# Delta rule: the masked blocks of the inversion levels made by GpSimd into two buffers, one level ahead

## The chip, the cores and the metric

The kernel runs on one core of one Trainium2 chip. The metric is the device time of one execution in microseconds (us). Engines are called PE (TensorE), DVE (VectorE), ACT (ScalarE), POOL (GpSimd) and SP (SyncE, which issues nearly all DMAs).

## The reference, cut to what matters

The whole program is two transformer blocks in fp32 on 256 tokens (gated linear attention, a feed-forward, stick-breaking attention, a mixture of experts, then a second block with a chunked gMLP beside a gated delta rule, a feed-forward, latent attention and a feed-forward). The change touches the gated delta rule alone, which runs over 512 tokens (256 of context, 256 of the sequence), four heads, in two directions:

```python
gcum = jnp.cumsum(gc, axis=-1)
decay = jnp.exp(jnp.where(tri_incl, gcum[..., :, None] - gcum[..., None, :], -jnp.inf))
a_mat = jnp.where(tri_strict, jnp.einsum('nbhid,nbhjd->nbhij', kb, kc) * decay, 0.0)
t_mat = lax.linalg.triangular_solve(eye + a_mat, eye, lower=True, unit_diagonal=True)
u = jnp.einsum('nbhij,nbhjd->nbhid', t_mat, vb)
```

The kernel inverts the unit triangular matrix block by block. It begins with 2x2 blocks and doubles the block size in five levels. A level takes the entries of the matrix that belong to it (a multiplication by a 0/1 mask), forms products with the inverse so far, and subtracts them.

## The kernel before, in words

The 512 tokens are four tiles of 128, and each direction (a `Strand`, d = 0 or 1) takes them in four steps, in its own order. Four heads lie side by side, as 64x64 blocks on two halves of the partitions. So a masked block is a 128x256 fp32 tile.

Three generators work for each strand:

- `prepare(x)` builds the matrix of a step with products on PE (L2318, L2365, L2380), DVE multiplications (L2337, L2327 in threes, L2372), GpSimd multiplications (L2358 and L2359 for the start `UM`, L2387 for the attention block) and ACT copies (L2346, L2393 for the start `TM`). The result goes to `x.pairs[step % 2]`. Its marks (the semaphore counts reached) are kept in `x.prepared[step]`.
- `invert(x)` runs the five levels. A level has: the masked block X; the first products X by TM (L2428, 16 matmuls a strand on PE, recorded as such); the ACT copy XT (L2437); the second products (L2462, L2465); two DVE subtractions (L2481 and L2483, or L2481 and L2486 twice at level 5). The mask multiplication of the next level stands on DVE (L2452) beside the ACT copy: it waits for the first products, since there is one buffer X, and its result is waited for by `after_all` in front of the second products and in front of the next first products. The mask of level 1 of the next step is made there too, if `x.prepared` already holds that step when the code reaches that point; if not, `masked` (L2410) makes it at the start of the step, followed by a `yield`.
- `follow(x)` carries the state: POOL L2507 and L2508, PE L2514, L2532, L2565, L2581, L2597, L2613, L2635 with DVE and ACT steps between them. L2565 needs the finished inverse of its step.

`side_by_side` takes the eight generators (the last two are `tail_norm`) in the order invert 0, invert 1, follow 0, follow 1, prepare 0, prepare 1, tails, and runs each to its next `yield`, round after round. The instruction order of every engine is the order in which this loop reaches the instructions, and each engine executes its queue in order. Taking out or adding one `yield` shifts a generator against the others by one round, on all engines. The generators of strand 1 begin three rounds later (`STAGGER`).

`after_all` waits for the latest count of each engine in the own generator's chain (`chain[-1]`); `adopt` adds other marks to it. Two waits in `prepare` use the global count: PE L2365 waits for `dve_done.n`, so for every DVE instruction emitted before it by any generator; DVE L2372 waits for `pe_done.n` in the same manner.

No weights are consumed in this stage. The DMA queue of SP has filled the ring before it and waits.

Of the kernel before, what the change touches and what calls it, by code (L numbers as in the profile page):

```python
# [15 lines left out]
ALU = mybir.AluOpType  # L16
# [47 lines left out]
def build(nc, stream, params, where, out):  # L64
# [4 lines left out]
    with ExitStack() as ctx:  # L69
# [3 lines left out]
        def sem(name):  # L73
            return ctx.enter_context(nc.semaphore(name))
# [17 lines left out]
        chain = [{}]  # L92
        tile_used = Done(sem("tile_used"), chain)
        pe_done = Done(sem("pe_done"), chain)
        act_done = Done(sem("act_done"), chain)
        dve_done = Done(sem("dve_done"), chain)
        pool_done = Done(sem("pool_done"), chain)
        everyone = (tile_used, pe_done, act_done, dve_done, pool_done)

        def after_all(eng):  # L100


            for d in everyone:
                n = d.n if len(chain) == 1 else chain[-1].get(d, 0)

                if n and not (len(chain) > 1 and eng.engine == nc.tensor.engine and d in (tile_used, pe_done)):
                    eng.wait_ge(d.sem, n)
# [17 lines left out]
        def c(name, a=0, b=None):  # L125
            off, n = where[name]
            return par[:, off + a:off + (n if b is None else b)]
# [18 lines left out]
        block = ctx.enter_context(nc.Block())  # L146
# [164 lines left out]
        def wait_marks(eng, marks):  # L311
            for d, n in marks:
                eng.wait_ge(d.sem, n)
# [1554 lines left out]
        W = GH * P  # L1868
# [17 lines left out]
        def marks_here():  # L1886
            return [(d, n) for d, n in chain[-1].items() if n]
# [4 lines left out]
        def adopt(*lists):  # L1892
            for marks in lists:
                for d, n in marks:
                    chain[-1][d] = max(chain[-1].get(d, 0), n)
# [371 lines left out]
        compact = lambda x: x.rearrange("p (h n) -> p h n", h=GH)  # L2267
        small_both = lambda m: m.unsqueeze(1).to_broadcast([P, GH, HB])
        ident_c = c("ident_c")
        CW = GH * HB  # L2270
# [124 lines left out]
                yield  # L2395

        def invert(x):
            X, TM = x.xt[:, 0:CW], x.xt[:, CW:W]
            UM, XT = x.ul[:, 0:CW], x.ul[:, CW:W]

            @block.gpsimd
            def _(pool):
                after_all(pool)
                pool_done.by(nc.gpsimd.memset(x.full, 0.0))

            def masked(step, lev):
                @block.vector
                def _(dve):
                    after_all(dve)
                    dve_done.by(nc.vector.tensor_tensor(compact(X), compact(x.pairs[step % 2][:, 0:CW]), x.level(lev), ALU.mult))  # L2410

            ahead = False
            for step in range(T4):
                while len(x.prepared) <= step:
                    yield
                adopt(x.prepared[step])
                if not ahead:
                    masked(step, 1)
                    yield
                for lev in range(1, 6):  # L2420
                    UM0, TM0 = (x.start[:, 0:CW], x.start[:, CW:W]) if lev == 1 else (UM, TM)

                    @block.tensor
                    def _(pe):
                        after_all(pe)
                        for n in range(GH):
                            for b_ in blocks2:
                                last = nc.tensor.matmul(ps[b_, x.b_level, hc_of(n)], X[b_, hc_of(n)], TM0[b_, hc_of(n)],  # L2428
                                                        start=True, stop=True)
                        pe_done.by(last)  # L2430
                    first_known = pe_done.n
                    yield

                    @block.scalar
                    def _(act):
                        after_all(act)
                        act_done.by(nc.scalar.activation(XT, ps[:, x.b_level, 0:CW], ACT.Copy))  # L2437
                    copied = act_done.n
                    if lev < 5:
                        masked_at, ahead = (step, lev + 1), True  # L2440
                    else:
                        masked_at, ahead = (step + 1, 1), len(x.prepared) > step + 1
                    if ahead:
                        if lev == 5:
                            adopt(x.prepared[step + 1])

                        @block.vector
                        def _(dve):
                            dve.wait_ge(pe_done.sem, first_known)
                            if lev == 5:  # L2450
                                wait_marks(dve, x.prepared[step + 1])
                            dve_done.by(nc.vector.tensor_tensor(compact(X), compact(x.pairs[masked_at[0] % 2][:, 0:CW]),  # L2452
                                                                x.level(masked_at[1]), ALU.mult))
                    yield

                    @block.tensor
                    def _(pe):
                        pe.wait_ge(act_done.sem, copied)
                        after_all(pe)
                        for n in range(GH):  # L2460
                            for b_ in blocks2:
                                nc.tensor.matmul(ps[b_, x.b_pair, hc_of(n)], XT[b_, hc_of(n)], UM0[b_, hc_of(n)],  # L2462
                                                 start=True, stop=True)
                            for b_ in blocks2:
                                last = nc.tensor.matmul(ps[b_, x.b_pair, hc_of(GH + n)], UM0[b_, hc_of(n)],  # L2465
                                                        XT[b_, hc_of(n)], start=True, stop=True)
                        pe_done.by(last)
                    yield
                    if lev == 1 and step:
                        while len(x.crossed) < step:  # L2470
                            yield
                        adopt(x.crossed[step - 1])
                    if lev == 5 and step:
                        while len(x.solved) < step:
                            yield
                        adopt(x.solved[step - 1])

                    @block.vector
                    def _(dve):
                        after_all(dve)  # L2480
                        last = nc.vector.tensor_tensor(TM, TM0, ps[:, x.b_pair, CW:W], ALU.subtract)  # L2481
                        if lev < 5:
                            last = nc.vector.tensor_tensor(UM, UM0, ps[:, x.b_pair, 0:CW], ALU.subtract)  # L2483
                        else:
                            for b_ in blocks2:
                                last = nc.vector.tensor_tensor(heads(x.full)[b_, :, b_], compact(UM)[b_],  # L2486
                                                               compact(ps[:, x.b_pair, 0:CW])[b_], ALU.subtract)
                        dve_done.by(last)
                    if lev == 1:
                        x.begun.append(marks_here())  # L2490
                    if lev == 5:
                        x.inverted.append(marks_here())
                    yield
# [196 lines left out]
        def tail_norm(half):  # L2690
# [30 lines left out]
            def _(dve):  # L2721
                after_all(dve)
                for t in range(2):
                    x = heads(osum[:, 2 * half + t, :])
                    last = nc.vector.tensor_tensor(x, x, vecs(root[:, GH * t:GH * t + GH]), ALU.mult)
                tail_scaled[half] = dve_done.by(last)

        side_by_side([invert(strands[0]), later(STAGGER, invert(strands[1])), follow(strands[0]), follow(strands[1]),
                      prepare(strands[0]), later(STAGGER, prepare(strands[1])), tail_norm(0), tail_norm(1)])

# [699 lines left out]
```

## Time and profile before

| | us |
|---|---|
| median of 3 runs (lowest, highest) | 2968.91 (2966.89, 2969.13) |
| the profiled execution, its own time | 2962.77 |
| its span, first to last instruction | 2961.0 |
| busy in the span: PE | 2787.0 (94%) |
| busy: DVE, ACT, POOL | 579.0, 358.2, 86.2 |

The delta rule's strands run from about 1818 us to 1983 us of the span. The inversion's first products run from 1829.2 us to 1972.4 us. DVE has 36 mask multiplications on L2452 and 4 on L2410 in that time. Idle time in brackets in a timeline row stands in front of the instruction; the name behind the arrow is the instruction that ended last among those it may have waited for.

### The profile page before, as it was taken

How to read it: one execution, taken by the hardware profiler on the slowest of the kernel's cores; microseconds unless marked ns; L12 is line 12 of the kernel's file. 1: busy time of each engine (PE TensorE's matmuls, PEld its weight loads, DVE VectorE, ACT ScalarE, POOL GpSimd, SP SyncE). 2: the span in 40 equal slices, each digit the busy share in tenths (PEclk: the TensorE clock that was granted, in tenths of full speed). 3: DMA queues.
4: the chain of work that ended last, by engine and by line, in shares of the span. 5: the costliest groups of instructions: out<-in, count | busy, mean ns of one | idle time of the engine just before them, and what ended most of it. 6: DMA issues, size and time to landing. Idle time of an engine off the chain costs nothing. (4 is left out here: it accounts for less than half of the span.)

```text
span 2961.0 us, 70141 instructions
## 1 busy us (share of the span) xinstructions
PE 2787.0 (94%) x31522; PEld 2062.2 (70%) x31522; DVE 579.0 (20%) x1419; ACT 358.2 (12%) x896; POOL 86.2 (3%) x129
## 2 busy tenths in 40 slices
PE   5899999989999999999998898989999999898999
PEld 2576865759899999999997545865444444545883
DVE  0021001112000000010001323652222201232331
ACT  0101001101000000000001211221111100121110
POOL 0000000000000000000000001210000000000000
PEclk9899999999999999999999899999999999999999
DMA  8893434328999999999994011001212221301432
GB/s 340 327 354 133 156 130 169 114 87 344 364 380 413 385 390 402 384 384 402 387 400 171 29 71 44 3 2 57 85 71 80 77 76 63 131 29 71 157 142 85
DMA packets 80391, 583.94 MB, mean 197 GB/s; under 512 B 8912, under 2 KB 8912, under 8 KB 10064
## 3 DMA queue, kind: packets, MB, share of 16 engines
q1 hardware_dynamic: 79920, 580.15, 50.1%
q8 instruction: 152, 2.49, 0.3%
q10 hardware_dynamic: 288, 1.05, 0.1%
q14 instruction: 31, 0.25, 0.0%
HBM read 580.11 MB, written 1.05 MB: 196 GB/s over the span
## 5 line engine op out<-in xcount | busy, mean ns | idle before, releaser
L1420 PE MATMUL ps<-arena,ring 128*64 128x88 f32 x14336 | 553.8, 240 | 22.2 <-issue 18.9
L1420 PEld LDWEIGHTS ps<-arena,ring 128*64 128x64 f32 x14336 | 548.4, 137 | 26.7 <-issue 24.7
L2779 PE MATMUL ps<-hT,ring 128*128 128x256 f32 (+2 forms) x1472 | 455.3, 472 | 5.6 <-ACT hT L471 3.4
L2779 PEld LDWEIGHTS ps<-hT,ring 128*128 128x128 f32 x1472 | 274.5, 190 | 185.2 <-issue 166.3
L358 PE MATMUL ps<-ring,arena 128*128 128x512 f32 x896 | 389.2, 595 | 4.9 <-DVE arena L2684 3.8
L358 PEld LDWEIGHTS ps<-ring,arena 128*128 128x128 f32 x896 | 170.5, 191 | 217.5 <-issue 211.3
L1429 PE MATMUL ps<-arena,ring 128*64 128x88 f32 x7168 | 274.7, 239 | 2.6 <-issue 2.6
L1429 PEld LDWEIGHTS ps<-arena,ring 128*64 128x64 f32 x7168 | 272.6, 137 | 3.3 <-issue 3.0
L1570 DVE TENSOR_TENSOR arena<-arena,ps 128x88 f32<-128x88 f32 x224 | 55.2, 247 | 512.1 <-ACT arena L1549 512.0
L930 PE MATMUL ps<-hT,ring 128*128 128x256 f32 (+1 forms) x736 | 152.7, 370 | 2.6 <-ACT hT L469 2.6
L1549 ACT ACTIVATE arena<-ps 128x88 f32<-128x88 f32 x224 | 54.7, 244 | 809.5 <-PE ps L1420 809.5
L930 PEld LDWEIGHTS ps<-hT,ring 128*128 128x128 f32 x736 | 134.8, 190 | 20.3 <-issue 3.0
L1928 PE MATMUL ps<-hT,ring 128*128 128x512 f32 x256 | 118.3, 618 | 0.0
L2824 DVE SCALAR_TENSOR_TENSOR arena<-ps,par,arena 128x510 f32<-128x510 f32 (+1 forms) x88 | 50.1, 611 | 300.3 <-ACT arena L2812 300.3
L1928 PEld LDWEIGHTS ps<-hT,ring 128*128 128x128 f32 x256 | 50.1, 199 | 59.5 <-issue 59.3
L575 PE MATMUL ps<-ring,arena 128*32 128x256 f32 x768 | 52.1, 432 | 35.7 <-DMA ring<-in_stream 35.7
L198 PE MATMUL ps<-hT,ring 128*128 128x256 f32 x352 | 79.5, 386 | 4.0 <-ACT arena L756 4.0
L2812 ACT ACTIVATE arena<-ps,par 128x512 f32<-128x512 f32 (+1 forms) x88 | 46.3, 577 | 278.5 <-PE ps L2779 278.5
L222 POOL TENSOR_TENSOR small<-small 128x1 f32<-128x1 f32 (+3 forms) x32 | 26.8, 838 | 1812.4 <-DVE small L418 1095.7
L198 PEld LDWEIGHTS ps<-hT,ring 128*128 128x128 f32 x352 | 67.4, 193 | 15.2 <-issue 6.1
L213 PE MATMUL ps<-ring,hT 128*128 128x512 f32 (+1 forms) x160 | 69.2, 592 | 0.0
L393 DVE TENSOR_TENSOR arena<-ps,arena 128x512 f32<-128x512 f32 x24 | 16.6, 692 | 260.6 <-PE ps L358 212.4
(462 smaller groups left out, 2115.5 us busy)
## 6 DMA issues: line engine op xcount, KB each, us to landing
ring<-in_stream SPq DMA_DIRECT2D x547, 1024.0 KB, 6.9
par<-in_params SPq DMA_DIRECT2D x1, 3397.0 KB, 28.5
h<-in_x ACTq DMA_DIRECT2D x2, 512.0 KB, 7.8
cx<-in_ctx SPq DMA_DIRECT2D x2, 512.0 KB, 29.4
out<-h SPq DMA_DIRECT2D x4, 256.0 KB, 2.0
par<-in_params SPq DMA_DIRECT2D x1, 941.0 KB, 6.0
```

The costliest lines, as they stand in the source:

```text
L198: last = nc.tensor.matmul(o[:, 0:ntok], w[:, k, half * P:half * P + P], src[:, k, tok0:tok0 + ntok], start=(k == 0), stop=(k == KT - 1))
L213: last = nc.tensor.matmul(ps[:, b, 0:cols], src[:, k, tok0 + n * P:tok0 + n * P + P], w[:, k - t0, 0:cols], start=(k == 0), stop=(k == kti ...
L358: last = nc.tensor.matmul(ps[:, b, :], src[:, k, t * P:t * P + P], w[:, k % kper, :], start=(k == 0), stop=(k == ktiles - 1))
L575: last = nc.tensor.matmul(ps[32 * j:32 * j + 32, 7, 0:256], cond[:, k, :], w, start=(k == 0), stop=(k == KT - 1))
L930: last = nc.tensor.matmul(ps[:, b, half * SEQ + tok.start:half * SEQ + tok.stop], w[:, k, half * P:half * P + P], hT[:, k, tok], start=(k ...
L1420: last = nc.tensor.matmul(ps[m:m + 64, up_bank[j], half * P:half * P + CAP], w[:, k, half * P + m:half * P + m + 64], hTe[:, k, :], start= ...
L1429: last = nc.tensor.matmul(ps[m:m + 64, 6 + q // 4, (q % 4) * P:(q % 4) * P + CAP], w[:, j, q * P + m:q * P + m + 64], hid[:, 2 * d + j, :] ...
L1549: nc.scalar.activation(sg[:, s % 2, :], ps[:, up_bank[s % RING], 0:CAP], ACT.Silu).then_inc(moe_silu, 1)
L1570: nc.vector.tensor_tensor(hid[:, s, :], sg[:, s % 2, :], ps[:, up_bank[s % RING], P:P + CAP], ALU.mult).then_inc(moe_hid[s % RING], 1)
L1928: last = nc.tensor.matmul(ps[:, banks[half], :], w[:, k, half * P:half * P + P], hT[:, k, :], start=(k == 0), stop=(k == KT - 1))
L2779: last = nc.tensor.matmul(ps[:, 2 * BANKS_CONV[f % RING] + half, tok], w[:, k, half * P:half * P + P], hT[:, k, tok], start=(k == 0), stop ...
L2824: nc.vector.scalar_tensor_tensor(seg(o, 1, SEQ), seg(x, 0, SEQ - 1), tap(0, half, f), seg(o, 1, SEQ), ALU.mult, ALU.add).then_inc(conv_lef ...
```

## The change

The mask multiplications leave DVE and are issued on GpSimd. There are two buffers in turn: the old one and a half of the parameter `ln_g`, which has been used up by then. At level `lev` the mask of `lev + 1` is issued ahead of the first products of `lev`. It waits for the first products of the level before, which used the same buffer. At level 5 the mask of the next step's level 1 is issued there if that step is already in `x.prepared`. This test now stands one `yield` earlier than before. A mask that could not be made ahead is issued at the start of the step, without the `yield` that followed. The chain of the generator does not take the mask's count up (`kept`), except by `adopt` in front of the first products. The second products lose their `after_all`.

```diff
         def invert(x):
-            X, TM = x.xt[:, 0:CW], x.xt[:, CW:W]
+            TM = x.xt[:, CW:W]
+            blocks_ = [x.xt[:, 0:CW], c("ln_g", CW * x.d, CW * x.d + CW)]
+            masked_to = lambda step, lev: blocks_[(5 * step + lev) % 2]
+            free_at = {}
...
             def masked(step, lev):
-                @block.vector
-                def _(dve):
-                    after_all(dve)
-                    dve_done.by(nc.vector.tensor_tensor(compact(X), compact(x.pairs[step % 2][:, 0:CW]), x.level(lev), ALU.mult))
-
-            ahead = False
+                at, kept = 5 * step + lev, chain[-1].get(pool_done, 0)
+
+                @block.gpsimd
+                def _(pool):
+                    if lev == 1:
+                        wait_marks(pool, x.prepared[step])
+                    if at > 2:
+                        pool.wait_ge(pe_done.sem, free_at[at - 2])
+                    known[at] = pool_done.by(nc.gpsimd.tensor_tensor(compact(masked_to(step, lev)),
+                                                                     compact(x.pairs[step % 2][:, 0:CW]), x.level(lev), ALU.mult))
+                chain[-1][pool_done] = kept
+
+            known = {}
             for step in range(T4):
...
-                if not ahead:
+                if 5 * step + 1 not in known:
                     masked(step, 1)
-                    yield
                 for lev in range(1, 6):
                     UM0, TM0 = (x.start[:, 0:CW], x.start[:, CW:W]) if lev == 1 else (UM, TM)
+                    X = masked_to(step, lev)
+                    if lev < 5:
+                        masked(step, lev + 1)
+                    elif len(x.prepared) > step + 1:
+                        masked(step + 1, 1)
+                    adopt([(pool_done, known[5 * step + lev])])
...
-                    first_known = pe_done.n
+                    free_at[5 * step + lev] = pe_done.n
                     yield
...
-                    if lev < 5:
-                        masked_at, ahead = (step, lev + 1), True
-                    else:
-                        masked_at, ahead = (step + 1, 1), len(x.prepared) > step + 1
-                    if ahead:
-                        if lev == 5:
-                            adopt(x.prepared[step + 1])
-
-                        @block.vector
-                        def _(dve):
-                            dve.wait_ge(pe_done.sem, first_known)
-                            if lev == 5:
-                                wait_marks(dve, x.prepared[step + 1])
-                            dve_done.by(nc.vector.tensor_tensor(compact(X), compact(x.pairs[masked_at[0] % 2][:, 0:CW]),
-                                                                x.level(masked_at[1]), ALU.mult))
...
                     def _(pe):
                         pe.wait_ge(act_done.sem, copied)
-                        after_all(pe)
```

## Rows read from the trace of the kernel before

**Rows 1.** Windows: length, busy PE, PEld, DVE, ACT, POOL, granted clock, DMA.
```profile
1818.00:1829.00 11.00, 6.22 (x56) 5.38 (x56) 6.90 (x18) 1.92 (x4) 4.09 (x6) 1.00 0.01 1
...
1896.90:1903.80 6.90, 3.99 (x123) 3.82 (x120) 5.03 (x11) 1.80 (x5) 1.27 (x1) 1.00 0.00 1
1903.80:1908.00 4.20, 4.20 (x55) 3.86 (x52) 1.80 (x5) 0.98 (x2) 0.00 (x0) 0.59 0.01 4
...
sum 165.00, PE 144.06 PEld 132.01 DVE 109.32 ACT 36.87 POOL 37.79; mean PE 14.41 PEld 13.20 DVE 10.93 ACT 3.69 POOL 3.78
```

**Rows 2.** One line's or tile's instructions: count, then min/median/max in ns.
```profile
L2452 DVE TENSOR_TENSOR arena<-arena,par x18: 408/426/1178, 1829.9 to 1963.4; 128x256 f32<-128x256 f32 x18
...
L2359 POOL TENSOR_TENSOR arena<-par,arena x4: 727/728/789, 1824.0 to 1929.6; 128x256 f32<-128x256 f32 x4
L2387 POOL TENSOR_TENSOR arena<-arena,par x4: 1262/1264/1276, 1826.7 to 1934.4; 128x512 f32<-128x512 f32 x4
```

**Rows 3.** Timeline of step 0's start: start, us, engine, line [idle before].
```profile
1828.75 0.94 POOL L2359 TENSOR_TENSOR par<-par 128x256 f32<-128x256 f32 x1
1829.20 0.68 PE L2428 MATMUL ps<-arena 64*64 64x64 f32 x16 [0.74 <-ACT arena L2393]
1830.74 1.27 POOL L2387 TENSOR_TENSOR hT<-hT,par 128x512 f32<-128x512 f32 x1 [1.05 <-PE ps L2380]
1832.13 0.39 ACT L2393 ACTIVATE par<-ps 128x256 f32<-128x256 f32 x1 [1.77 <-POOL hT L2387]
...
1833.23 0.68 PE L2428 MATMUL ps<-par 64*64 64x64 f32 x16 [1.47 <-DVE par L2410]
```

**Rows 4.** Timeline, levels 4 and 5 of step 0.
```profile
1847.77 1.18 DVE L2327 TENSOR_TENSOR hT<-hT,ps 64x256 f32<-64x256 f32 x3
1848.77 1.26 POOL L2387 TENSOR_TENSOR arena<-arena,par 128x512 f32<-128x512 f32 x1 [3.93 <-PE ps L2380]
1848.99 1.33 DVE L2452 TENSOR_TENSOR par<-hT,par 128x256 f32<-128x256 f32 x1
1850.37 1.16 PE L2365 MATMUL ps<-arena 128*128 128x128 f32 x8 [1.28 <-DVE par L2452]
...
1853.44 0.68 PE L2380 MATMUL ps<-par 64*64 64x64 f32 x16
```

**Rows 5.** Timeline: a DVE subtraction with a PSUM operand beside a GpSimd instruction.
```profile
1854.25 0.41 DVE L2483 TENSOR_TENSOR hT<-hT,ps 128x256 f32<-128x256 f32 x1
1854.26 1.27 POOL L2387 TENSOR_TENSOR par<-par 128x512 f32<-128x512 f32 x1 [2.49 <-PE ps L2380]
```

**Rows 6.** Timeline, end of step 1 and start of step 2.
```profile
1898.43 0.47 PE L2565 MATMUL ps<-arena 64*64 64x64 f32 x5 [1.46 <-ACT par L2437]
...
1899.51 1.27 POOL L2387 TENSOR_TENSOR hT<-hT,par 128x512 f32<-128x512 f32 x1 [3.20 <-PE ps L2380]
...
1899.67 0.28 PE L2462 MATMUL ps<-par 64*64 64x64 f32 x4
...
1902.51 0.47 PE L2565 MATMUL ps<-par,hT 64*64 64x64 f32 x5 [1.45 <-ACT hT L2437]
...
1903.84 1.87 PE L2597 MATMUL ps<-hT 128*128 128x128 f32 x8
```

**Rows 7.** Timeline, end of step 2 and start of step 3.
```profile
1939.05 0.68 PE L2380 MATMUL ps<-par 64*64 64x64 f32 x16
...
1940.90 0.47 PE L2565 MATMUL ps<-arena 64*64 64x64 f32 x5 [0.51 <-issue]
...
1942.79 0.33 PE L2462 MATMUL ps<-par 64*64 64x64 f32 x4 [0.95 <-ACT hT L2437]
```

**Rows 8.** Timeline, levels 4 and 5 of step 3.
```profile
1968.74 0.38 ACT L2437 ACTIVATE par<-ps 128x256 f32<-128x256 f32 x1 [5.37 <-PE ps L2428]
1969.17 0.41 DVE L2452 TENSOR_TENSOR par<-hT,par 128x256 f32<-128x256 f32 x1
...
1969.84 0.33 PE L2462 MATMUL ps<-par 64*64 64x64 f32 x4 [0.73 <-ACT hT L2437]
```

## The prediction

> **What bounds the kernel now.** I read the page's shares first: PE is busy for 94% of the span, so a change off PE can only win back PE's idle time. I then took the windows around the strands, the timeline of PE alone for the bracketed idle times, and the timelines of all engines around each of them. The windows [rows 1] show the stage: 165 us, of which PE works 144.1, so 21 us are idle. That is the ceiling for any change here, 0.7% of the whole. DVE is busy for 109 us and POOL for 38, so neither is full. PE's queue is in order and mostly dense. The idle time sits in a few places: the start of step 0 [rows 3], the end of each step, where L2565 waits for the finished inverse [rows 6, 7], and single waits [rows 4, 8]. So what counts is not how long 40 masks take, but which of these places has a mask in its last wait, and which will have one. The view of DMA matters for nothing here; its share is 0.01 [rows 1].
>
> **The order, counted from the code.** Because every engine's order is fixed by the yields, I counted rounds for both versions. In steps 0 and 1 PE's order stays the same: the yield that is dropped moves strand 0 one round earlier, and strand 1, which begins three rounds later, likewise. From the first products of step 2 on, the two inversions run one round earlier against the other generators, until the last level of step 2. There PE's L2380 of strand 1's step 3 moves from ahead of L2565 to behind it, which is the arrangement that step 2 has already. The test for "already prepared" now fails for step 3 as well: prepare reports it one round too late. So masks of level 1 that are not ahead are needed for steps 0, 2 and 3 in both strands (before: 0 and 2). For strand 0 such a mask stands on POOL behind L2387 of strand 1 in steps 2 and 3, and ahead of PE's first products of the step.
>
> **Part 1, the instruction itself.** A mask took 0.43 us on DVE (median 426 ns, but up to 1178 ns). GpSimd did the same shape, two SBUF inputs, in 0.73 us (L2359) [rows 2]. I take 0.73. Forty of them add 29 us to POOL's 38 in a stage of 165, so POOL is not filled. A mask made ahead has a whole level of its strand to be ready, 146 us / 20 = 7 us on average, and behind the longest POOL entry in its way (L2387, 1.26) it is still early. In dense stretches this part costs PE nothing. If that cover failed and each first product had to wait for the difference, 40 x 0.3 = 12 us would be added. At the other end, relieving DVE of 17 us gains nothing there either, because PE has no idle time to give back.
>
> **Part 2, the start of step 0: a loss.** POOL is busy until 1829.69 with L2359 of strand 1; 0.2 of that is drawn out by the DVE mask beside it, so say 1829.5. The mask then ends at 1830.25 and the first products start at 1830.4 instead of 1829.20: +1.2. L2380 and so L2387 (before: 1830.74) follow 1.15 later, ACT's L2393 too. From its end to the first products of strand 1 it took 0.71 (1832.52 to 1833.23), and will take 0.15 + 0.73 + 0.1 = 1.0. That gives 1834.6 instead of 1833.23, a loss of 1.4 us, and PE is dense behind it [rows 3].
>
> **Part 3, L2365: two gains.** At 1850.37 PE had been idle for 1.28 us. The last real need, the threes of L2327, was met at 1848.95, but the global DVE count also took in a mask, which took 1.33 us beside a GpSimd instruction [rows 4]. With no mask on DVE the gap is gone: -1.28. The same wait, 1.28 long, stands once more at 1935.98. In exchange POOL has a mask between L2387 and L2358: shifted by 1.4, L2387 ends at 1851.45, the mask at 1852.2, L2358 and L2359 (0.73 each) at 1853.7. PE's L2380, which reads their result, could start at 1853.6 and does at 1853.85: +0.25.
>
> Beside that GpSimd instruction a DVE instruction with a PSUM operand kept its 0.41 us [rows 5]. The Trainium skill, "SBUF — State Buffer", on the port pair that VectorE and GpSimd share, says that a VectorE instruction with two SBUF inputs and a GpSimd instruction exclude each other for their whole length. By that rule the move ends the collisions, since DVE's other work in this stage nearly all reads PSUM. A plainer reading, that any GpSimd work holds up VectorE, would put up to 29 us on DVE; the trace speaks for the rule.
>
> **Part 4, the start of step 2: a loss.** L2565 and L2380 run as before; L2387 runs 1899.51 to 1900.78. The mask ends at 1901.5, the first products run 1901.65 to 1902.25, and the second products of strand 1, level 5, start then instead of at 1899.67: +2.6. Before, L2565 of strand 1 came 2.84 after them, at 1902.51, with 1.45 of idle PE ahead of it. About 0.3 of that was a stretched mask on DVE. Now the second products of strand 0 come ahead of L2565 and fill part of the wait. L2565 comes at 1902.25 + 2.5 = 1904.8 and ends near 1905.2, where the same work was done at 1903.84 before: +1.35 [rows 6].
>
> **Part 5, the start of step 3: a net loss.** Level 5's second products of strand 0 ended at 1939.05; without the gap of part 3 they end at 1937.8. In the arrangement of step 2 L2565 came about 2.0 after that point, so at 1939.8. L2380 ends 0.9 later, at 1940.7, L2387 at 1942.15, the mask at 1942.9. The first products end at 1943.65 and strand 1's second products start then, instead of at 1942.79: +0.85, with the second 1.28 of part 3 already in it [rows 7].
>
> **Part 6, smaller gains.** At 1969.84 the second products waited for a mask that had stood on DVE behind other work (1969.17 to 1969.58), while their ACT copy was ready at 1969.12. Without `after_all` they start at about 1969.25: -0.6 [rows 8]. A GpSimd L2508 ahead of step 1's L2514 was drawn out by 0.15 to 0.2 by a DVE mask: -0.15. The other idle times before L2565 (0.5 to 1.0 each) hang on the DVE subtractions after the second products, with no mask in between, and stay. The waits dropped in front of the second products cost nothing where PE is dense.
>
> **The sum.** 1.4 - 1.28 + 0.25 - 0.15 + 1.35 + 0.85 - 0.6 = +1.8 us. Against the profiled execution's 2962.77 us that makes 2964.6. The runs' median lies 6.1 above that execution, so I predict 2968.91 + 1.8 = 2970.7 us. What this measurement can tell from no change is about 0.2%, 5.9 us: the forecast is "no difference".
>
> **Rival A, faster.** GpSimd's masks do not stand in the way at the starts (it runs them earlier than I count, or PE finds other work), and only the gains are left: 2 x 1.28, 0.6, 0.3 and 0.15, 3.6 in all, giving 2965.3. If the idle stretch before 1903.8 shrinks too, PE keeps the full clock that it lost there: 4.2 us were run at 0.59, near the lower level of 1.2 GHz [rows 1], which is worth 4.2 x 0.41 = 1.7. Then it is 2963.6. For it: DVE's relief is real. Against it: the position of the level-1 masks behind L2387 is in the code, and the wait on them is unconditional.
>
> **Rival B, slower, by the clock.** PE's clock fell right after the stretch in which it was idle for 2.9 of 6.9 us [rows 1]. The starts of steps 0, 2 and 3 all get longer idle stretches (2.45 in one piece in step 2). If each brings one more stretch like that, it is 3 x 1.7 = 5.1 on top of 1.8: 2975.8, slower by 0.23%. It decides at whether the clock after the starts of steps 0 and 3 stays at 1.0. Against it: between 1818 and 1829 PE was busy for only 6.2 of 11 us and the granted clock stayed at 1.00 [rows 1]. With one more stretch it is 2972.4. The Trainium skill, "TensorE: Matmul & The Clock Gate", Part 1, has the clock fall to half after an idle period and rise after sustained work; by it longer idle stretches speak for this rival, and the row from 1818 shows that idling of this size need not bring it.
>
> **Rival C, late masks in dense stretches.** POOL waits in order, on PE and ACT, in L2387 and L2507, and a mask behind them comes too late in more places than the starts: up to the 12 us of part 1, 2977 with half of them. I find at least 2 us of slack at each.
>
> **Chances.** Forecast (0 to +3.5) 0.57; A 0.2; B 0.17, of which a third beyond 5.9 us; C 0.06. The likeliest one's own range is 2968.5 to 2972.5. For 8 in 10 I take in A's first number and B's second step and C's beginning: 2965.0 to 2976.0. Faster by more than 0.2% needs A with the clock and a shift of the runs' level: 0.04. Slower by more than that: B's end and C, with the same shift: 0.1. Same: 0.86.
>
> **What would show it.** After: no DVE multiplication on two SBUF operands between 1829 and 1975; 40 POOL multiplications of 0.73; PE's idle time before L2365 gone in both places; first products of steps 0, 2 and 3 released by a POOL mask, with gaps near 1.9 before the first (0.74 before), 2.4 in step 2 and 2.3 in step 3; and L2462 near 1969 not waiting. The forecast is wrong if the level-1 masks end before L2387 of the other strand, if L2565 of step 3 does not come some 2.0 after the second products of strand 0, or if the granted clock falls below 1 anywhere but once in this stage.

## The result, and the profile after

The changed kernel took 2975.88 us (median of 11 runs, 2973.01 to 2979.16), the kernel before 2966.89 us (median of 11, 2960.82 to 2970.53). The ratio is 1.0029 with a 95% interval of 1.0021 to 1.0037: slower by 8.6 us, 6 to 11. Two later sets, on two chips, gave 1.0015 (1.0002 to 1.0028) and 1.0024 (1.0009 to 1.0038). So it is slower each time, by 0.15% to 0.29%. The profiled execution took 2976.43 us.

The page's first part shows that the work has moved as meant: DVE has 40 instructions fewer, POOL 40 more, and PE is busy for 8 us more with the same number of matmuls.

```profile
span 2974.4 us, 70063 instructions
...
PE 2795.3 (94%) x31522; PEld 2067.1 (69%) x31522; DVE 559.5 (19%) x1379; ACT 357.9 (12%) x896; POOL 112.7 (4%) x169
```

More busy time for the same matmuls is the first hint of the clock. Windows of the changed kernel, with the columns of [rows 1]; first the strands, then four pieces of them. Strands are counted from here on from the start of the first L2318 to the start of the last products of `follow` (L2635, here L2634); in the kernel before that is 1813.3 to 1981.4, a little more than the 165 us of the prediction:

```profile
1819.90:1991.30 171.40, 148.24 (x2697) 136.17 (x2697) 90.64 (x250) 38.01 (x99) 69.03 (x83) 0.96 0.03 9
1828.80:1832.20 3.40, 3.21 (x15) 2.72 (x14) 2.31 (x6) 0.63 (x1) 1.46 (x2) 0.52 0.02 5
1838.80:1842.20 3.40, 2.83 (x48) 2.67 (x48) 0.38 (x2) 0.38 (x1) 1.28 (x2) 0.51 0.00 0
1910.70:1914.10 3.40, 3.40 (x78) 3.40 (x76) 1.40 (x4) 0.38 (x1) 2.00 (x3) 0.52 0.03 5
1951.70:1955.10 3.40, 3.29 (x70) 3.32 (x72) 0.37 (x2) 0.38 (x1) 2.70 (x4) 0.52 0.03 5
```

The kernel before needed 168.1 us for its strands and had one such piece, after 1903.8 [rows 1]. Here there are four, in which PE ran at its lower level, 1.2 GHz. The whole span is 13.4 us longer than in the first profile of the kernel before (2974.4 against 2961.0), the strands only 3.3; the other 10.1 lie where the code is the same, and the section on the prediction comes back to them.

The masks on GpSimd, by the view of one line; 40 of them, as cheap as L2359 had been [rows 2]:

```profile
L2418 POOL TENSOR_TENSOR par<-hT,par x20: 722/727/737, 1842.2 to 1974.2; 128x256 f32<-128x256 f32 x20
L2418 POOL TENSOR_TENSOR par<-arena,par x10: 720/724/740, 1836.6 to 1958.7; 128x256 f32<-128x256 f32 x10
L2418 POOL TENSOR_TENSOR arena<-arena,par x10: 721/725/729, 1837.3 to 1968.4; 128x256 f32<-128x256 f32 x10
```

Line numbers have shifted: first products are L2443, second products L2461 and L2464, the ACT copy L2452, and what was L2565 is L2564. The start of step 0, answering to [rows 3], in order of time:

```profile
1836.57 0.72 POOL L2418 TENSOR_TENSOR par<-arena,par 128x256 f32<-128x256 f32 x1
...
1837.44 0.68 PE L2443 MATMUL ps<-arena,par 64*64 64x64 f32 x16 [1.82 <-POOL par L2418]
...
1838.16 0.69 DVE L2372 TENSOR_TENSOR hT<-hT,ps 128x512 f32<-128x512 f32 x1 [3.76 <-PE ps L2443]
...
1838.95 1.12 PE L2380 MATMUL ps<-par 64*64 64x64 f32 x16 [0.83 <-ACT hT L2452]
...
1843.05 0.68 PE L2443 MATMUL ps<-par 64*64 64x64 f32 x16 [1.28 <-POOL par L2418]
```

Levels 4 and 5 of step 0, answering to [rows 4]: L2365 has no idle time in front of it any more, and L2380 waits 0.17 for GpSimd.

```profile
1857.58 1.19 DVE L2327 TENSOR_TENSOR hT<-hT,ps 64x256 f32<-64x256 f32 x3
...
1858.83 1.16 PE L2365 MATMUL ps<-arena 128*128 128x128 f32 x8
1859.80 0.73 POOL L2418 TENSOR_TENSOR par<-arena,par 128x256 f32<-128x256 f32 x1
...
1862.16 0.53 PE L2380 MATMUL ps<-par 64*64 64x64 f32 x11 [0.17 <-POOL par L2359]
```

The start of step 2, answering to [rows 6]: the mask stands behind L2387, ends at 1909.95, and the first products wait for it. The ACT copy L2393 in front of them had ended at 1909.76 and was no longer in the way.

```profile
1906.92 0.47 PE L2564 MATMUL ps<-arena 64*64 64x64 f32 x5 [1.46 <-ACT par L2452]
...
1908.01 1.26 POOL L2387 TENSOR_TENSOR hT<-hT,par 128x512 f32<-128x512 f32 x1 [3.21 <-PE ps L2380]
1909.23 0.72 POOL L2418 TENSOR_TENSOR par<-arena,par 128x256 f32<-128x256 f32 x1
...
1910.10 0.76 PE L2443 MATMUL ps<-arena,par 64*64 64x64 f32 x16 [2.23 <-POOL par L2418]
```

The start of step 3, answering to [rows 7], is now a copy of it, and the first products run at half clock (1.12 us instead of 0.68):

```profile
1948.64 0.47 PE L2564 MATMUL ps<-arena 64*64 64x64 f32 x5 [1.46 <-ACT par L2452]
...
1951.81 1.12 PE L2443 MATMUL ps<-arena 64*64 64x64 f32 x16 [2.23 <-POOL arena L2418]
...
1956.02 0.47 PE L2564 MATMUL ps<-par,hT 64*64 64x64 f32 x5 [0.18 <-issue]
```

Near the end of step 3, answering to [rows 8], the second products no longer wait (a row without brackets has no idle time in front of it):

```profile
1979.77 0.33 PE L2461 MATMUL ps<-par 64*64 64x64 f32 x4
```

### The profile page after: what moved, and what is told of

Read it like the earlier page. It is cut to its first block and busy times, and to the rows that moved or that the text cites. A ratio compares the mean times of both kernels' runs of the same rounds, so it can differ in the third digit from the quotient of the medians.

```text
span 2974.4 us, 70063 instructions
## 1 busy us (share of the span) xinstructions
PE 2795.3 (94%) x31522; PEld 2067.1 (69%) x31522; DVE 559.5 (19%) x1379; ACT 357.9 (12%) x896; POOL 112.7 (4%) x169
## 5 line engine op out<-in xcount | busy, mean ns | idle before, releaser
L575 PEld LDWEIGHTS ps<-ring,arena 128*32 128x32 f32 x768 | 27.8, 123 | 54.3 <-issue 43.1
```

The source lines that it names most:

```text
L575: last = nc.tensor.matmul(ps[32 * j:32 * j + 32, 7, 0:256], cond[:, k, :], w, start=(k == 0), stop=(k == KT - 1))
```

## The experiments

Every profile was read in the same way: the length of the strands, PE's idle time within it, and how long PE ran at half clock there (windows of 0.5 us, clock below 1, added up). Lengths and idle times are good to 0.1 us. "In prepare" means that `prepare` issues the level-1 mask, right where its input is made; "filled" means products that nobody reads, put into an idle time of PE. The last three columns are of one execution each. Sets were run at different times on different chips, so a kernel is compared first with the runs of its own set.

| kernel | ratio to the kernel before (95%) | strands, us | PE idle in them, us | half clock in them, us |
|---|---|---|---|---|
| before | 1 | 168.1 | 22.5 | 3.4 |
| before, second profile | (one run) | 170.8 | 22.3 | 10.2 |
| changed | 1.0029 (1.0021 to 1.0037) | 171.4 | 23.2 | 13.7 |
| changed, second | 1.0015 (1.0002 to 1.0028) | 177.9 | 22.8 | 30.7 |
| changed, third | 1.0024 (1.0009 to 1.0038) | 171.4 | 23.2 | 13.7 |
| changed, old order | 0.9993 (0.9984 to 1.0002) | 169.1 | 20.2 | 13.7 |
| changed, level-1 masks on DVE | 0.9997 (0.9987 to 1.0007) | 167.3 | 22.3 | 3.4 |
| changed, idle filled | 0.9996 (0.9987 to 1.0005) | 168.4 | 20.5 | 0 |
| changed, level-1 masks in prepare | 0.9972 (0.9958 to 0.9986) | 161.8 | 17.7 | 3.4 |
| before, no wait of second products | 0.9983 (0.9975 to 0.9992) | 166.4 | 21.1 | 3.4 |
| before, two narrowed waits | 0.9985 (0.9973 to 0.9997) | 162.2 | 18.6 | 0 |
| the same, level-1 masks in prepare | 0.9979 (0.9968 to 0.9990) | 163.0 | 17.9 | 3.4 |
| before, L2565 filled | 1.0010 (1.0000 to 1.0020) | 167.4 | 19.0 | 3.4 |
| two narrowed waits, in prepare, filled | 0.9992 (0.9981 to 1.0003) | 163.4 | 15.3 | 3.4 |

### The changed kernel again

> The changed kernel once more, for the spread of its time and of its clock between executions. Theory: ratio 1.0029 again, 4 half-clock stretches between the start of the strands and their end, as in its first profile. Rival (the second half of the difference came from stretches outside the delta rule that differ from run to run): ratio nearer 1.0015 and another number of half-clock stretches.

Measured: 1.0015, and in its profile the most half clock of all, 30.7 us of 177.9. The idle times are those of the first profile to within 0.1 us, but for some ahead of step 0's first products, where slower matmuls filled them. So the order and the waits are the same each time and the clock is not. The ratio is the one that the rival named: this execution's strands were 6.5 us longer than the first one's, and its whole was 4.3 us shorter (span 2970.1 against 2974.4). So the time outside the strands, where the code is that of before, moves by 11 us between two executions. The third set, whose expectation follows, gave 1.0024, and its profile 13.7 us in four stretches, as expected.

> The changed kernel a third time, beside the run with the filled waits. Theory: 1.0015 to 1.0029, 4 or more half-clock stretches within the strands.

### The order of before, masks on GpSimd

```diff
                 if 5 * step + 1 not in known:
                     masked(step, 1)
+                    yield
...
                     if lev < 5:
                         masked(step, lev + 1)
-                    elif len(x.prepared) > step + 1:
-                        masked(step + 1, 1)
...
                     copied = act_done.n
+                    if lev == 5 and len(x.prepared) > step + 1:
+                        masked(step + 1, 1)
                     yield
```

> The changed kernel with the yields and the place of the 'already prepared' test as they were before: the order of PE is that of the kernel before, the masks stay on GpSimd, one level ahead, two buffers. Theory (waits for a level-1 mask at the starts of steps 0, 2 and 3, each followed by a stretch of half clock): the start of step 3 goes back to idle times of about 0.5 and 0.1 us instead of 1.46 and 2.23, and its half-clock stretch goes: 3.5 to 5 us less than the changed kernel, ratio to the kernel before 1.0012 to 1.0018. Rival (it is the masks on GpSimd as such, anywhere): stays at 1.0029. Rival (something outside this stage): stays at 1.0029.

Measured: 0.9993. Step 3 is as forecast; the mask is ahead, and idle times of 0.41 and 0.21 stand where 1.46 and 2.23 stood. PE's timeline there:

```profile
1948.38 0.47 PE L2565 MATMUL ps<-arena 64*64 64x64 f32 x5 [0.41 <-issue]
...
1949.54 0.33 PE L2462 MATMUL ps<-par 64*64 64x64 f32 x4 [0.21 <-ACT par L2451]
```

No half clock followed in step 3. Of the 13.7 us in the rest of the strands 3.4 came before the first products of step 0, and 10.2 behind the waits for a mask that remained at the starts of steps 0 and 2 (1.84 and 2.23). The ratio is 5 us better than I expected, but I had counted from 1.0029, and in this set the changed kernel itself had 1.0015 (2972.04 us). Against that the run is 3.9 us faster by the medians and 4.8 by the means (1.7 to 7.9), as the expected 3.5 to 5. The strands of the profiles are 2.3 us shorter than the changed kernel's first. The sign and the place are shown, the size only roughly. L2380 in step 0, which waits 0.83 in the changed kernel, does not wait here.

### Level-1 masks on VectorE, the others on GpSimd

```diff
                 if 5 * step + 1 not in known:
-                    masked(step, 1)
...
+                    @block.vector
+                    def _(dve):
+                        after_all(dve)
+                        if at > 2:
+                            dve.wait_ge(pe_done.sem, free_at[at - 2])
+                        dve_done.by(nc.vector.tensor_tensor(compact(masked_to(step, 1)), compact(x.pairs[step % 2][:, 0:CW]),
+                                                            x.level(1), ALU.mult))
...
```

> The changed kernel, but the level-1 masks that are not made ahead (steps 0, 2 and 3 of both strands, 6 of 40) are made by VectorE as in the kernel before; the other 34 stay on GpSimd; the order of PE is that of the changed kernel. Theory (only the 6 masks behind another GpSimd instruction cost): all of the loss goes but what the order costs, about 0 to +1 us against the kernel before, ratio 0.9990 to 1.0005. Rival (the new order costs by itself, step 3 arranged as step 2): +2 to +4 us, 1.0010. Rival (GpSimd masks in dense stretches cost): 1.0025.

Measured: 0.9997. With 34 of 40 masks on GpSimd and the changed order no loss is left that could be told; the changed kernel of this set is 4.7 us slower by the means (1.3 to 8.1). So the loss hung on the six level-1 masks, and GpSimd in the dense stretches costs nothing that these runs can tell. The 1.46 before L2565 in step 3, which the new order brings, is still there (L2573 in this kernel, below), but the strands are 167.3 us long with 22.3 us of idle PE, as in the kernel before:

```profile
1940.00 0.47 PE L2573 MATMUL ps<-arena 64*64 64x64 f32 x5 [1.46 <-ACT par L2461]
```

### Idle time filled: the clock by itself

```diff
                     masked(step, 1)
+                    fill = {(0, 0): 2, (1, 0): 2, (0, 2): 3, (0, 3): 3}.get((x.d, step), 0)
+
+                    @block.tensor
+                    def _(pe):
+                        for n in range(GH * fill):
+                            for b_ in blocks2:
+                                nc.tensor.matmul(ps[b_, x.b_level, hc_of(n % GH)], ident_c[b_, :], ident_c[b_, :],
+                                                 start=True, stop=True)
```

> The changed kernel with extra products (64x64, identity by identity, into a bank that the next first products overwrite) on PE ahead of the waits for a level-1 mask: two groups of 16 in both strands at step 0, three in strand 0 at steps 2 and 3. They take 1.2 and 1.8 us of idle times of 1.3 to 2.2 us, so nothing should move but the clock. Theory (the longer idle stretches lower the clock, which costs about 1.7 us a time): fewer half-clock stretches in the delta rule, at most 2 where the changed kernel had 4 and more, and 3 to 7 us less than the changed kernel, ratio 1.0000 to 1.0012. Rival (the idle time itself is all the loss, the clock falls by chance): the same number of stretches and the same time, 1.0015 to 1.0029.

The extra products write a bank that the next first products overwrite. Everything else, with every wait for GpSimd, is as in the changed kernel. Measured: 0.9996, that is 2967.7 us beside 2975.22 us of the changed kernel in the same set (medians; the means are 6.8 apart, 3.5 to 10.1). The whole strands ran at full clock; the window over them, and the waits that are still there:

```profile
1818.50:1986.90 168.40, 147.89 (x2856) 135.83 (x2856) 90.58 (x250) 38.01 (x99) 69.06 (x83) 1.00 0.03 9
```

```profile
1946.54 1.27 POOL L2387 TENSOR_TENSOR par<-par 128x512 f32<-128x512 f32 x1 [3.21 <-PE ps L2380]
1946.81 0.98 PE L2435 MATMUL ps<-par 64*64 64x64 f32 x28
1947.76 0.72 POOL L2418 TENSOR_TENSOR arena<-arena,par 128x256 f32<-128x256 f32 x1
...
1948.63 0.68 PE L2451 MATMUL ps<-arena 64*64 64x64 f32 x16 [0.84 <-POOL arena L2418]
```

L2451, the first products of step 3, still wait for the mask; only PE has something to do (L2435) in the meantime. This decides between the theories. The waits are all in place, 7.5 us are gone, and the strands' clock is 1.00 where it was 0.96. The mean granted clock of the listed runs of this set says so too: 0.9786 for the filled kernel, 0.9754 for the changed one. The profiles show less of it than the medians: the strands are 3.0 us shorter than in the changed kernel's profile of this set, and the two profiled executions took the same time (2968.5 and 2968.22 us), the latter being among the fastest of its kernel. Where the other 4.5 us lay, no profile shows. The run also gives the price of the waits alone: 168.4 us without any half clock, against 168.1 - 1.7 = 166.4 for the kernel before if its 3.4 us at half clock are taken off at full PE load. The waits cost 2.0 us of the strands. That the rest of the loss is the clock's is taken from the runs' times, and not seen in full in one profile.

### Level-1 masks by GpSimd in prepare

```diff
+                self.first = c("ln_b", CW * d, CW * d + CW)
...
                     pool_done.by(nc.gpsimd.tensor_tensor(compact(UM), small_both(ident_c), compact(UM), ALU.subtract))
+                kept = chain[-1][pool_done]
+
+                @block.gpsimd
+                def _(pool):
+                    pool_done.by(nc.gpsimd.tensor_tensor(compact(x.first), compact(Atc), x.level(1), ALU.mult))
+                chain[-1][pool_done] = kept
...
-                if 5 * step + 1 not in known:
-                    masked(step, 1)
+                known[5 * step + 1] = chain[-1][pool_done]
...
```

> The changed kernel, but the level-1 masks are made by GpSimd in prepare, right behind L2359 and so ahead of L2387 of the other strand, in buffers of their own (the two halves of ln_b); 40 masks on GpSimd, PE's order that of the changed kernel. Theory (what costs idle time is the place of the level-1 mask in GpSimd's queue, not the engine): no first product waits for a mask; the 2.2 us idle times at steps 2 and 3 split into 0.5 and 1.0 further on as in the run with VectorE's level-1 masks; strands 166 to 167.5 us at full clock, ratio 0.9990 to 1.0000. Rival (masks on GpSimd late in any place): waits for GpSimd masks stay, 1.0015 or more.

The level-1 mask has a buffer of its own here (`x.first`), so it need not wait for a free one; the lines left out give the other masks their two buffers and waits. Measured: 0.9972, the best ratio of all (2957.19 us, only 6 runs), though its interval overlaps those of the three kernels near 0.998. It is better than I expected: the strands took 161.7 us and not 166 to 167.5. PE is idle for 4.8 us less than in the kernel before. 2.6 of that are the two waits in front of L2365, about 0.9 the second wait at the start of step 2, where the expected 1.0 did not come, and 0.7 the wait of [rows 8]; the rest is small and has both signs. All 40 masks are on GpSimd, and PE's order is that of the changed kernel. Step 2 in its timeline (L2568 is what was L2565, L2447 the first products, L2394 what was L2387, L2425 the masks of levels 2 to 5, L2465 the second products):

```profile
1897.27 0.47 PE L2568 MATMUL ps<-arena 64*64 64x64 f32 x5 [1.46 <-ACT par L2456]
...
1898.05 0.63 PE L2447 MATMUL ps<-arena,par 64*64 64x64 f32 x16
1898.36 1.27 POOL L2394 TENSOR_TENSOR hT<-hT,par 128x512 f32<-128x512 f32 x1 [2.52 <-PE ps L2387]
...
1900.45 0.33 PE L2465 MATMUL ps<-arena,hT 64*64 64x64 f32 x4 [0.55 <-ACT hT L2456]
```

The first products start 0.3 us before L2394, behind which their mask used to stand in the queue. The place in GpSimd's queue was the fault, and the engine was not.

### The kernel before with its waits narrowed

```diff
                         pe.wait_ge(act_done.sem, copied)
-                        after_all(pe)
```

> The kernel before with one edit of the change alone: no after_all in front of the second products; masks stay on VectorE in one buffer. Theory: only the waits near the end of step 3 are shorter, -0.6 us, ratio 0.9998, not to be told from 1. Rival (the wait costs PE at each of 20 levels a strand): -2 us or more, 0.9993.

Measured: 0.9983, strands 166.4. Both waits for a mask in front of second products went ([rows 7], 0.95, and [rows 8], 0.73), 1.7 us together; I had counted one of them. The time of the whole fell by 5 us (2.4 to 7.4). That is the size that the rival named, but its place is not: in the strands only these two waits and small changes are seen, and the profile does not show where the rest lies.

```diff
                 def _(pe):
-                    pe.wait_ge(dve_done.sem, dve_done.n)
+                    pe.wait_ge(dve_done.sem, chain[-1][dve_done])
```

> The kernel before with two waits narrowed and nothing moved: no after_all in front of the second products, and L2365 waits for its own strand's VectorE count in place of the global one. Theory: the 0.73 and 0.95 us near the end of the strands go as in the run with the first edit alone (1.6 us of the strands' 168.0), and both 1.28 us waits in front of L2365 go as well: strands' length 163.9 us, ratio 0.9980 to 0.9986. Rival (the 1.28 come back behind L2365 as waits for strand 1's mask): 166.4 as with the first edit alone, ratio 0.999.

Measured with both edits: 0.9985, strands 162.2. The two 1.28 us are gone and no other wait took their place. Of the 4.2 us between these strands and those of the first edit alone, 2.6 are these waits and up to 1.7 the half clock that did not come in this profile. The time of the whole does not tell the two kernels apart (0.9983 and 0.9985), so the gain of the second edit is seen in the strands alone:

```profile
1817.50:1979.70 162.20, 143.60 (x2696) 131.47 (x2696) 109.94 (x290) 37.81 (x100) 42.34 (x43) 1.00 0.03 9
```

> As the run with two narrowed waits, and the level-1 masks are made by VectorE in prepare, right behind the values that they multiply, in a buffer of their own; the yields stay, so that PE's order is that of the kernel before. Theory (at a step's start only the mask's wait for its turn is to be saved, ACT's copy is ready earlier): idle before the first products of step 0 0.74 -> 0.15 and 1.47 -> 0.85, so 1.2 us less than the run with two narrowed waits, nothing at the later starts; ratio 0.9975 to 0.9983. Rival (a VectorE instruction more in prepare delays its chain as much): the same as with the two narrowed waits.

This run made the level-1 masks on DVE behind L2327's products of prepare, `nc.vector.tensor_tensor(compact(x.first), compact(Atc), x.level(1), ALU.mult)`, in a half of `ln_g`. Measured: 0.9979, strands 163.0 of which 3.4 at half clock (1.7 us), so 0.9 less than the run before it at full clock, where 1.2 were expected. Its interval overlaps those of the two kernels above it.

### Idle time filled in front of L2565

```diff
+                before_inverse = dict(chain[-1])
                 adopt(x.inverted[step])
...
+                    for d in (act_done, dve_done, pool_done):
+                        if before_inverse.get(d, 0):
+                            pe.wait_ge(d.sem, before_inverse[d])
+                    for n in range(GH * {(0, 0): 1, (0, 1): 2, (1, 1): 2, (0, 3): 1, (1, 3): 1}.get((x.d, step), 0)):
+                        for b_ in blocks2:
+                            nc.tensor.matmul(ps[b_, x.b_level, hc_of(n % GH)], ident_c[b_, :], ident_c[b_, :],
+                                             start=True, stop=True)
                     after_all(pe)
```

> The kernel before with extra products ahead of L2565 in the idle times there (one group of 0.6 us where 0.68 and 0.95 were idle, two groups where 1.45 were), into a bank that is overwritten later; nothing else is changed. Theory (each idle stretch of PE is a chance for a half-clock stretch): the one that the kernel before had behind step 1's end goes, -1 to -2 us, ratio 0.9993 to 0.9997, hardly told from 1. Rival (that stretch comes anyway, from somewhere earlier): 1.0000 or, where the extra products are in the way, 1.0005.

> The run with the level-1 masks in prepare and the two narrowed waits, plus the same extra products ahead of L2565. Theory: all strands at full clock, 161 to 162 us, ratio 0.9975 to 0.9980, the best of all. Rival (its clock needs no help): 0.9979 again or a little more from products in the way.

The products have a wait of their own, for what the generator had made before it took up the inverse. Measured: 1.0010 and 0.9992, where the kernels that were filled have 1 and 0.9979. The first is slower by 3 us, just clear of the noise; the second is from another set than its 0.9979, and the intervals overlap (0.9981 to 1.0003, 0.9968 to 0.9990). The half clock at step 2's start of the kernel before did not appear in its profile, which is what the theory says, but one ahead of step 0's first products did. In the strands PE's idle time fell by 3.5 and 2.6 us and its busy time rose by 2.8 and 3.0, so hardly anything was won there. The loss of the whole is not seen in the strands and stays unexplained. Filling paid in the waits of the changed kernel, where the clock was lost each time, and not here.

> The kernel before once more, for a second profile. Theory: the same idle times to 0.1 us in the strands and 0 to 2 half-clock stretches there, against 4 and more in the changed kernel.

Measured: idle times as in the first profile to 0.02 us, but 10.2 us at half clock, three times the first profile's. They are two stretches, 3.4 us at the start of step 2 as before and 6.8 from 1980.5 on, so within the 0 to 2 that I expected.

## Why the prediction was right or wrong

The time lay in the range, 0.1 us below its upper edge, and there was luck in that: of the two later sets of the same kernel one had 2972.04 us. The forecast, +1.8 us and no difference that could be told, did not hold. Rival B's mechanism did. That its number, 2975.8, is what came, is luck as well. B adds 6.9 to a base of 2968.91, and the larger set had the kernel before at 2966.89, with 8.6 more for the changed one. B also prices three further stretches at 1.7 us each. Three came, but only those at the starts of steps 0 and 3 were new in the places that it named: step 2 had its stretch before already, and the third came ahead of step 0's first products. And the strands of that profile were 3.0 us longer than the filled ones, not 5.1. Point by point:

- **Order.** The order of PE counted from the yields was right throughout, with step 3 arranged as step 2 and the level-1 masks of strand 0 behind L2387 in both (in step 0 it stands behind L2359).
- **Part 1** was right: 0.73 us each, and nothing lost in dense stretches (the run with 34 of 40 on GpSimd).
- **Part 2**, the start of step 0: the first products' idle time rose from 0.74 to 1.82, as forecast. One term was missing. DVE's L2372 waits for the global PE count. With the `yield` gone the first products are issued ahead of it, so it waited for them, and L2380 waited for it: 0.83 (the row's bracket names the ACT copy, but that ended at 1838.58 and L2372 at 1838.85). With the old order there is no such wait. Idle in front of the three instructions went from 2.21 to 3.93, +1.7 instead of +1.4.
- **Part 3** was right: both 1.28 gone, 0.17 for L2380 instead of 0.25. That L2462 behind it would wait 0.2 longer (1.16 instead of 0.95) was missed.
- **Part 4** put 2.45 for the wait at step 2; it was 2.23. The wait that I expected in front of strand 1's L2565 did not come, since the second products of strand 0 filled it. So +0.8 idle instead of +1.35.
- **Part 5** was right: 3.07 of idle time before, 3.87 after, +0.8 for 0.85.
- **Part 6** was right in both items.
- **The sum** of the idle times is +2.0 us by the filled run, for 1.8. It was right as a sum of waits.
- **The step that failed** is the clock. I left it out of the sum, at nothing, and gave rival B 0.17. I set against it one row, the stretch from 1818 to 1829, where PE idled and kept its clock [rows 1]. It was one execution's luck: in 8 of the 14 profiles the clock fell within some 9 us of the strands' first products, behind a wait of 2.0 to 2.7 us in front of L2318 that all 14 have, the kernel before too. The runs put the clock at about 5 us of a loss of 6.7 (below), and filling the waits gave back 7.5.

What the profiles show of rival B is a chance, not a threshold. At step 0's first products PE waited 1.8 us or more for a level-1 mask in the three profiles of the changed kernel and in that with the old order, and 2.2 for one in that with DVE's; half clock followed in 5 of 5. In the 9 other profiles the waits were shorter or filled: 0 of 9. At step 2 it followed in 4 of 4 with a wait of 2.2, in 3 of 5 where the longest was 1.3 to 1.5 in both of two places, and in 0 of 5 where these were filled or mostly gone. At step 3 in 3 of 3 with the changed kernel, and in 0 of 11 others. That idling lowers the clock is what the filled run shows, at 7.5 us. The rule of the Trainium skill, "TensorE: Matmul & The Clock Gate", Part 1, that the clock is halved after idling, agrees. The same page of the Trainium skill also says that the point at which the clock rises varies from run to run; here single profiles of one kernel differ in the time at half clock (13.7, 30.7 and 13.7 us), and no run shows whether that is the reason.

The mean granted clock of whole runs says the same without a profile. It is listed to three digits for each run: 0.9755 on average over the 33 runs of the changed kernel, 0.9779 over 90 of the kernel before, and 0.9786 over the 11 of the filled one. A clock of one half for h us lowers the mean over 2970 us by h / 5940, so 0.0024 means 14 us more at half clock, and up to half of that, 7 us, in time. A straight line of time on clock, fitted to the 123 runs of the two kernels, gives 2.1 us for each 0.001. By it the two kernels' means, 6.7 us apart, differ by 5.0 with the clock, and at equal clock the changed kernel is 1.7 us slower (0.2 to 3.2; with the sets kept apart 1.2, -0.5 to 2.8). That is a correlation, but it meets the forecast's 1.8 and the filled run's 2.0 for the waits.

What stays open: the three profiles of the changed kernel have strands 4.1 us longer on average (173.6) than the two of the kernel before (169.5), of some 6.7 us (the mean of the three sets). Outside the strands, where the code is the same, they took 2803.0, 2792.2 and 2794.7 us, and the two of the kernel before 2792.9 and 2798.8: 0.7 us apart on average, with a spread of up to 11 us within one kernel. So the 10.1 us outside the strands in the first pair of profiles are no effect that repeats, and five profiles are too few to place the last 2 to 3 us.

## What to carry to other kernels

- When work goes to another engine, look at what stands ahead of it in that engine's queue at the few places where PE already waits, not at its busy share. Here 34 masks moved without effect, and 6 brought the loss; with the level-1 masks issued right where their input was made, all 40 on the same engine gave 0.28% (0.14% to 0.42%) against the kernel before.
- A wait added to PE has two prices, its length and a chance of a stretch at 1.2 GHz behind it. The second was the larger here, by the fitted line three to one. Read the granted clock from several profiles, or from the listed runs, before a wait is called safe. Dummy products in the wait are worth a try, and a measurement: they gave 7.5 us in one kernel and cost 3 us in another.
- A wait for "everything issued so far" on another engine, written where only one result is needed, is a hidden link between independent strands: L2365's cost 2.6 us of the strands, and L2372's passed on a delay of 0.8.

## What the runs showed of the hardware that was not expected

- Matmuls that nobody reads, put into waits of 1.3 to 2.2 us, made a kernel 7.5 us faster (medians of one set). The strands' granted clock rose from 0.96 to 1.00.
- With the waits the same to 0.1 us, three executions of one kernel on three occasions spent 13.7, 30.7 and 13.7 us of the strands at half clock, worth up to 6.5 us between them (171.4 and 177.9).
